# Latent attention: convolution's projection chunks two places sooner, two score units beside the last chunk

## The reference, cut to what matters

```python
def latent_mix(p, kv_ctx, cos, sin, qk_g, rpb, conv_w, rows):
    qa, qb, pkv, cx, cb, cc = jnp.split(p, PROJ_SPLIT, axis=-1)      # p = u @ w_in
    ka, va, kb, vb = split_kv(pkv, qk_g[1])
    qa = apply_axial_rope(rms_norm(heads(qa, A_Q_HEADS), qk_g[0]), cos, sin)
    ka = apply_axial_rope(ka, cos, sin)
    o_a = gqa_attention(qa, [ka, ka_ctx], [va, va_ctx])              # 6 heads
    o_b = neighbourhood_attention(qb, kb, vb, kb_ctx, vb_ctx, rpb)   # 6 heads, with a bias
    o_c = short_conv_mixer(cx, cb, cc, conv_w)                       # cb * conv(cc * cx), 3 taps, 256 channels
    return jnp.concatenate([o_a, o_b, o_c], axis=-1)                 # then @ w_o
```

## Time and profile before

| | |
|---|---|
| runs | 2932.14, 2931.88, 2928.0 us (median 2931.88) |
| profiled execution, its own time | 2929.26 us |
| its span | 2927.5 us |
| mean granted clock of PE | 0.976 |
| PE busy | 2833.6 us (97%) |
| PE weight loads | 2349.2 us (80%) |
| DVE busy | 1776.2 us (61%) |
| ACT busy | 1161.6 us (40%) |
| POOL busy | 161.4 us (6%) |
| layer 0: chunk at place 9, end, and attention's end | 1639.49, 1650.41, 1717.33 us |
| layer 1: the same | 2645.29, 2651.05, 2694.45 us |

### The profile page before, as it was taken

One profiled execution on the slowest core, in us unless ns is written; L12 is line 12 of the kernel. 1 busy time (PEld: TensorE's weight loads), 2 busy tenths in 40 slices (PEclk: granted clock), 3 DMA queues, 4 the chain that ended last, 5 costly groups with the idle time before them and its releaser, 6 DMA issues.

```text
span 2927.5 us, 39349 instructions
## 1 busy us (share of the span) xinstructions
PE 2833.6 (97%) x16472; PEld 2349.2 (80%) x16472; DVE 1776.2 (61%) x2622; ACT 1161.6 (40%) x1556; POOL 161.4 (6%) x146
## 2 busy tenths in 40 slices
PE   6999999998999999999999998999999999999999
PEld 5887678786867787888888678888888888896998
DVE  4555359756643787837662577737668466636544
ACT  3433347534433664222332563222342223436544
POOL 0000000000000000000030132000020000301000
PEclk8999999999999999999999998999989999999999
DMA  8648789846377994444423112434425344231353
GB/s 315 244 174 315 274 304 368 303 165 282 144 273 262 345 356 170 177 139 162 152 93 101 44 44 87 184 134 179 137 82 201 133 160 158 101 109 69 138 187 112
DMA packets 77329, 539.72 MB, mean 184 GB/s; under 512 B 8688, under 2 KB 8944, under 8 KB 16736
## 3 DMA queue, kind: packets, MB, share of 16 engines
q1 hardware_dynamic: 75728, 530.92, 49.0%
q0 software_dynamic: 1424, 6.28, 0.8%
HBM read 536.12 MB, written 1.05 MB: 183 GB/s over the span
## 4 chain that ended last, share of the span: by engine, by line
PE 90%; DVE 5%; DMA 2%; ACT 2%; issue 1%; POOL 0%; SPq 0%; DVEq 0%; ACTq 0%
PE bank L1114 10%; PE bank L1428 10%; PE bank L1429 10%; PE bank L1430 10%; PE bank L1309 4%; PE bank L1463 4%; PE bank L1464 4%; PE bank L1465 4%; PE bank L1311 4%; PE bank L1310 4%; PE bank L1619 2%; PE bank L1334 2%; DMA raw<-in_w_mods 2%; PE bank L1336 2%; PE bank L1301 2%; PE bank L1335 2%
## 5 line engine op out<-in xcount | busy, mean ns | idle before, releaser
L2343 DVE TENSOR_TENSOR w_lo<-raw,w_hi 128x2048 fp32r<-128x2048 f32 (+1 forms) x351 | 772.0, 2201 | 328.9 <-ACT w_hi L1799 314.8
L1799 ACT ACTIVATE w_hi<-raw 128x2048 fp32r<-128x2048 f32 (+1 forms) x351 | 644.8, 1839 | 517.1 <-PE bank L1465 207.2
L1428 PE MATMUL bank<-h_hi,w_hi 128*128 128x512 f32 (+1 forms) x1472 | 527.7, 358 | 13.4 <-DVE h_lo L2521 9.8
L1430 PE MATMUL bank<-h_hi,w_lo 128*128 128x512 f32 (+1 forms) x1472 | 524.7, 356 | 0.0
L1429 PE MATMUL bank<-h_lo,w_hi 128*128 128x512 f32 (+1 forms) x1472 | 524.7, 356 | 0.0
L1428 PEld LDWEIGHTS bank<-h_hi,w_hi 128*128 128x128 f32 x1472 | 281.3, 191 | 56.6 <-DVE h_lo L2521 9.0
L1430 PEld LDWEIGHTS bank<-h_hi,w_lo 128*128 128x128 f32 x1472 | 281.4, 191 | 38.8
L1429 PEld LDWEIGHTS bank<-h_lo,w_hi 128*128 128x128 f32 x1472 | 281.5, 191 | 38.3
L2395 DVE CUSTOM_DVE_ANT_0 bank<-raw,raw 128x1024 f32<-128x1024 f32 x240 | 286.4, 1257 | 0.0
L2099 ACT ACTIVATE quads<-bank 128x512 f32<-128x512 f32 (+1 forms) x88 | 47.9, 544 | 567.3 <-PE bank L1430 567.3
L1463 PE MATMUL bank<-act_hi,w_hi 128*128 128x512 f32 (+1 forms) x594 | 219.6, 370 | 0.0
(11 more groups left out here) (508 smaller groups left out, 4646.1 us busy)
## 6 DMA issues: line engine op xcount, KB each, us to landing
raw<-in_w_experts SPq DMA_DIRECT2D x192, 1024.0 KB, 6.5
raw<-in_w_ffn_in SPq DMA_DIRECT2D x88, 1024.0 KB, 4.8
raw<-in_w_mods SPq DMA_DIRECT2D x60, 1024.0 KB, 7.4
raw<-in_w_wide SPq DMA_DIRECT2D x60, 1024.0 KB, 4.8
raw<-in_w_ffn_out SPq DMA_DIRECT2D x48, 704.0 KB, 4.1
raw<-in_w_c_in SPq DMA_DIRECT2D x20, 1024.0 KB, 4.8
raw<-in_w_a_in SPq DMA_DIRECT2D x12, 1024.0 KB, 5.9
raw<-in_w_b_in SPq DMA_DIRECT2D x12, 1024.0 KB, 6.1
```

What stands on the lines that cost most here:

```text
L1428: pe.matmul(o, hi[:, f, :], h_hi[:, k, cols], start=(k == 0), stop=False)
L1430: mm = pe.matmul(o, lo[:, f, :], h_hi[:, k, cols], start=False, stop=(k == KT - 1))
L1799: act.activation(w_hi[pair_of(k)][:, 0:size], raw_of(k)[:, 0:size], ACT.Copy).then_inc(sem("hi_ready"), 1)
L2343: dve.tensor_tensor(w_lo[pair_of(k)][:, 0:size], raw_of(k)[:, 0:size], w_hi[pair_of(k)][:, 0:size].bitcast(F32), ALU.subtract).then_inc(*r ...
```

## The change

The three chunks of the convolution go two places ahead, chunks 5 and 2 go last. POOL starts when chunk 9 has been copied at place 7, and does the nine operations of both halves before it waits for the first upper part; the upper parts are taken at units 3 and 5 (layer 0) and 2 and 4 (layer 1). The scores' banks change places: 4 and 5 for even units, 0 and 1 for odd. PE does the scores of unit 0 ahead of the first item of the last chunk, and those of unit 1 ahead of its second item; the waits for `roped` 3 and `dup` 1 go there too. DVE's queue has no new place for the two maxima: they are the first of its attention, behind the split of the next weights. ACT does the first exponential between the wait for the last item's product and the copy of that item.

```diff
-        IN_ORDER = (4, 6, 3, 0, 1, 5, 2, 7, 8, 9)
+        IN_ORDER = (4, 6, 3, 0, 1, 7, 8, 9, 5, 2)
-        CONV_AT = ((9, 15), (4, 8))
+        CONV_AT = ((3, 5), (2, 4))
+        score_bank = lambda u: 4 * ((u + 1) % 2)
...
-                pool.wait_ge(*W("evac_a", (9, 1), at=f"in{l}"))
+                pool.wait_ge(*W("evac_a", (in_at(9), 1), at=f"in{l}"))
...
                     pool.tensor_tensor(g_cb[:, n, 0:nq], out_, g_cb[:, n, 0:nq], ALU.mult).then_inc(*T("conv", n))
+                for n in range(2):
                     pool.wait_ge(*W("conv_upper", n))
...
                         for n, it in enumerate(items):
+                            if name[:2] == "in" and c == len(ITEMS[name]) - 1:
+                                latent_scores(int(name[2]), n)
+                                stage[0] = name
                             bank_ready(bank_of(name, c, n))
...
+            def latent_scores(l, u):
+                stage[0] = f"mix2.{l}"
+                s, pair, qb = units(l)[u]
+                k0, k1 = keys_of(s)
+                if u == 0:
+                    pe.wait_ge(*W("mix_v", ("roped", 3), at=f"in{l}"))
+                    pe.wait_ge(*W("mix_a", ("dup", 1), at=f"in{l}"))
+                if u == 1:
+                    bank_ready(0)
+                    bank_ready(1)
+                if u >= 2:
+                    pe.wait_ge(*W("mix_a", ("exp", u - 2)))
+                for x in range(2):
+                    half = slice(64 * x, 64 * x + 64)
+                    k = g_kd[half, (2 * pair + x) // 3, k0:k1] if pair < 3 else g_kb[half, pair - 3, k0:k1]
+                    mm = pe.matmul(psum[score_bank(u) + x][:, 0:k1 - k0], g_q[half, pair, T1 * s + P * qb:T1 * s + P * qb + P], k,
+                                   start=True, stop=True)
+                mm.then_inc(*T("product", ("scores", u)))
+
             def attention(l):
                 stage[0] = f"mix2.{l}"
-                pe.wait_ge(*W("mix_v", ("roped", 3), at=f"in{l}"))
-                pe.wait_ge(*W("mix_a", ("dup", 1), at=f"in{l}"))
-                for b in range(4):
-                    bank_ready(b)
                 us = units(l)
-                for u in range(len(us) + 4):
+                for u in range(2, len(us) + 4):
                     if u < len(us):
...
+                        latent_scores(l, u)
+                    if u == 3:
+                        bank_ready(2)
+                        bank_ready(3)
...
                             act.wait_ge(*W("product", (c, n)))
+                            if (name[:2], c, n) == ("in", len(chunks) - 1, 1):
+                                latent_exp(int(name[2]), 0)
+                                stage[0] = name
                             evac(c, n).then_inc(*T("evac_a", (c, n)))
...
+            def latent_exp(l, u):
+                stage[0] = f"mix2.{l}"
+                k0, k1 = keys_of(units(l)[u][0])
+                act.wait_ge(*W("mix_v", ("max", u)))
+                for x in range(2):
+                    ins = act.activation(g_p[u % 3][:, x, 0:k1 - k0], psum[score_bank(u) + x][:, 0:k1 - k0], ACT.Exp,
+                                         bias=g_st[u % 2][:, x:x + 1], accum_out=g_st[u % 2][:, 2 + x:3 + x])
+                ins.then_inc(*T("mix_a", ("exp", u)))
+
             def attention(l):
...
-                for u in range(len(us) + 4):
+                for u in range(1, len(us) + 4):
```

## The result

The changed kernel takes 2920.59 us in the median of 7 runs (2915.39 to 2923.64), the kernel before, measured beside it, 2929.51 us (7 runs). The ratio is 0.9966, 95% interval 0.9956 to 0.9976: it is faster by 0.3%, 9 us between the medians and 10 by the ratio. The forecast was 2929.0 us, with 2924.0 as the lower end of the range.

The account below looks back on a forecast made before the run. PE, 90% of the chain of waits, was taken to bound the kernel. Layer 0's -1.6 and layer 1's -1.0 us, with one clock fall of 1.4, gave -1.2, so 2929.1, stated as 2929.0 us; range 2924.0 to 2934.0.

Parts of the forecast that it names:

- The sum without a clock fall: Touched places of both layers with PE's clock staying up: -1.6 us in layer 0, -1.0 in layer 1, -2.6 together.
- The wait ahead of the last chunk: PE waits for the rotation and doubled key before the last projection chunk: 0.7 us lost in each layer.
- The blocked rotation: Before layer 0's last chunk, POOL blocks two DVE rotation steps: 0.9 us lost, ends 0 and 2.3; layer 1: 0.
- The two score units: Scores of units 0 and 1 inside the projection: 1.06 to 1.14 us each, 2.2 us later per layer.
- The first output: Attention's first output product ends 8.9 us behind the last chunk, before 13.0 and 12.6: gains 4.1 and 3.8 us.
- The table load: ACT's load before the first exponential falls ahead of the last chunk's end, costing nothing; rival uncovered: +2.6 us, chance 0.1.
- DVE's scalings without POOL: In the attention, with POOL gone: 1.3 us come back in layer 0, where DVE sets the pace, 0.1 in layer 1.
- One fall at the attention's start: PE's clock falls once in the two layers behind the last chunk: costs 1.4 us, leaving -1.2 of -2.6.
- item (5): Both chunk orders, loads and splits: same sizes, split ends more than 1 us before it is needed; nothing.
- the chance of 0.07 for a gain of over 0.2%: Whole kernel faster by over 0.2%, with 5.9 us as what can be told from no change: chance 0.07.

Follow-up runs that it names:

- scores alone: Kernel before plus the change's early scores and first exponential, with the old chunk order and old convolution: 2928.01 us, ratio 0.9993.
- convolution alone: Kernel before plus the change's chunk order, POOL convolution and upper-part places, with scores, maxima and first exponential as before: 2928.18 us, ratio 0.9995.
- 0.9984 with 7 fillers: Kernel before with 7 extra 128-column matmuls on PE behind the attention of layer 0, nothing else changed: 2926.07 us, ratio 0.9984.
- the one with 7 fillers: Changed kernel with 7 extra 128-column matmuls on PE behind the attention of layer 0: 2928.4 us, ratio 1.0003.

## Why the prediction was wrong, step by step

**The touched places: right.** The sum without a clock fall was -1.6 in layer 0 and -1.0 in layer 1, -2.6 us; the trace has -1.96 and -0.44, -2.4 us. By terms:

- The wait ahead of the last chunk, 0.7 us in each layer: the scores start 0.76 us behind the doubling's matmul (1645.63 against 1644.87), and what ends the wait is the copy of the doubled key. Right.
- **The blocked rotation, 0.9 us: it was 0.** The three steps took their 0.41 and 0.42 us, although POOL's tensor_scalar (1643.92 to 1645.49) ran beside all of them. A little later DVE's split, also with two operands in SBUF, took 3.00 us beside POOL's tensor_tensor at 1646.88, against 2.29 us in the kernel with the scores alone. In the earlier trace rows, from which I took the 1.75 us, POOL's operation was a tensor_tensor as well. In all nine profiles with the convolution moved it is the same (one step of an earlier rotation, 0.54 us, is the most that the tensor_scalar did). So what I took for "POOL works" was one of its kinds, and the rotation met the other. The order counts as well: where DVE's split started first (1629.85) it took its 2.29 us, and POOL's two tensor_tensor behind it took 3.16 us instead of 1.23. The rule that I quoted from the Trainium skill (page "SBUF — State Buffer", section "Who interferes with whom") makes no such difference between POOL's operations that read SBUF, and both kinds do; the rotation's rows speak against it for POOL's tensor_scalar, the split's for it with the tensor_tensor. Which step meets which is chance here: no experiment moved them against each other.
- The two score units, 2.2 us: 1.13 and 1.06 and **0.45 us that I had not priced**. The chunk was one piece of 10.90 us and is now 5.67 + 5.70 = 11.37. Layer 1 shows it too: 5.76 against 3.05 + 3.08 = 6.13. The kernel with the scores alone has 5.64 + 5.70 for the same chunk, the one with the convolution alone 10.94 in one piece. So it comes with the scores between the halves; why stays open. T comes later by 3.4 us in layer 0 (forecast 3.8) and 3.3 in layer 1 (2.9).
- The first output, T + 8.9 and T + 8.8: 8.85 and 2658.18 - 2649.19 = 8.99. Right. In layer 0 ACT is late next, as said: the chain goes through both pairs of exponentials and the copy between them. In layer 1 it goes another way for the same time: unit 2's scores, its maximum (2651.90) and its exponentials.
- The table load: at 1653.08, right behind the copy of the item before and 6 us ahead of T, as the earlier trace rows let expect. With the waits the other way round it cost 2.6 us by itself and 5.5 with the falls of the clock that it brought. The Trainium skill's page "ScalarE: Activation LUTs" (section "What ACT_TABLE_LOAD costs") says about 2.66 us for a switch, of which about 1.28 us are the load itself and the rest a drain. The load agrees (1.28 us); no drain shows here, for in the open the exponential stood 0.02 us behind the load.
- DVE's scalings without POOL, -1.3 and -0.1: from the first output to the end of the attention layer 0 goes from 53.95 to 52.67, layer 1 from 30.79 to 30.65. Right.
- One fall at the attention's start, +1.4 us: there was none, in either layer (granted clock 1.00 from 1659 to 1664 and from 2649 to 2660). I had taken one of the two possible falls, because the new still time lay between the rows that I had, and it went the better way. The price itself was a little low: 1.6 us in layer 0 of the kernel before.

**The step that failed is the sum's scope.** "The sum. Layer 0 ... Layer 1 ... Together -2.6 us, if PE's clock stays up" counts the clock at the two touched places alone, and item (5), "Nothing", is the last term. Nothing in the sum stands for the work behind the touched places, and no reason is given for leaving it out. The terms outside were in the trace: 47.7 us at half clock between B and D, behind waits of PE that the change leaves as they are but moves by 2 us. At 0.42 us each, an estimate from the difference of the two kernels, that is 20 us of time which the clock's falls hold, and it moved by 8.6: 4.2 in the first join and 4.4 in the second. No rival had a place outside the touched stretches, the range was made of the terms inside with the spread of the runs, and the chance of 0.07 for a gain of over 0.2% had no mechanism outside them behind it. A mechanism of this kind has no sign: another sum of the same size might have cost 1 us more (convolution alone, 881.56) or given 9. What could have been worked out from the trace of before was the width, not the value: three falls of 10 to 14 us. What such a fall moved by when it shrank was 4.2 to 4.4 us in the joins above, so some 4 us each, with either sign for new ones.

**What stays open.** Why the joins are long at 149.0 us and short at 146.9 or 149.9 the runs don't say. They show that the position of the later work decides and the change as such does not; from what the position counts, and why 150.02 and 150.07 us differ, they don't show. Single executions vary, so a median (0.9984 with 7 fillers) moves less than one profile (7 us). And the gain of the change is for the most part one of position: the changed kernel with 4 us of other edits ahead of the joins may have it or lose it, as the one with 7 fillers lost it. None of the kernels tried is measurably faster than the changed one.

## What to carry to other kernels

When PE runs at half clock anywhere in the trace, a change that moves later work by 1 or 2 us can gain or lose several times what it does where it stands: add up the half-clock time behind the touched place, price it by a pair of equal rows at both clocks (an upper end, for a fall is cheaper where others than PE set the pace), and put that into the range with both signs. Judge an edit by the stretch that it touches, cut at rows that both kernels have, and test a gain from elsewhere with a few fillers in the kernel before: if work added gives the same gain, it is position and not merit. If an ACTIVATE needs a new table and two waits, write the wait that is met early last, right ahead of it: in the traces here that one becomes the instruction of its own, with the load behind it. Then look in the trace where the load fell.

## What the runs showed of the hardware that was not expected

- 1.0 us of matmuls added between two stages made the kernel before faster (2926.07 against 2929.68 us, ratio 0.9984), and 1.0 us added to the changed one made it 8 to 9 us slower (2928.4 against 2920.59 and 2919.28).
- POOL's tensor_scalar (1.57 us, 128x512) did not slow DVE's tensor_tensor with two SBUF operands (0.41 us); POOL's tensor_tensor did (3.00 against 2.29 us), and was itself slowed where DVE's started first (3.16 against 1.23 us for two).
- Two matmul groups of another kind between the halves of a chunk cost 0.4 us beyond their own time.
- A table load placed by the order of two waits: 6 us ahead of the exponential, or 1.28 us in the open and 3.2 us in all with the fall of the clock.
- A fall of the clock for 6.8 us cost 0.5 us in a join where the chain went through DVE for half of it (86.32 against 85.85 us), and 3.4 us of it cost 1.6 us where PE worked through.
